# Expert weights in whole units of 2 MB, and hidden activations turned in 64x64 quarters, in a two-layer encoder on one core

## What is computed

```python
# t: tokens x 1024.  w_gate, w_up: 4 x 4 experts x 1024 x 512.  w_down: 4 x 4 x 512 x 1024
gates = g_onehot[:, :, None] * (g_w[:, None] * e_gate)[:, None, :]   # top group, then its top 2 experts
out = jnp.zeros_like(t)
for gi in range(MOE_GROUPS):
    hg = jnp.einsum('td,edf->tef', t, w_gate[gi])
    hu = jnp.einsum('td,edf->tef', t, w_up[gi])
    act = jax.nn.silu(hg) * hu * gates[:, gi, :, None].astype(t.dtype)
    out = out + jnp.einsum('tef,efd->td', act, w_down[gi])
```

## Time and profile before

| | us |
|---|---|
| median of 3 runs | 730.15 |
| lowest and highest of them | 729.17 and 730.3 |
| the profiled execution | 729.28 |
| its span, first to last instruction | 727.5 |

### The profile page before, as it was taken

One profiled execution on the slowest core, in us unless ns is written; L12 is line 12 of the kernel. 1 busy time (PEld: TensorE's weight loads), 2 busy tenths in 40 slices (PEclk: granted clock), 3 DMA queues, 4 the chain that ended last, 5 costly groups with the idle time before them and its releaser, 6 DMA issues.

```text
span 727.5 us, 8400 instructions
## 1 busy us (share of the span) xinstructions
PE 707.7 (97%) x3182; PEld 329.6 (45%) x3182; DVE 277.8 (38%) x683; ACT 149.2 (21%) x365; POOL 26.4 (4%) x47
## 2 busy tenths in 40 slices
PE   9999999999999999989999999999999999998996
PEld 6488454564333333333445545464333333332344
DVE  1213361544427242422322557363435424242224
ACT  3000241341111111110331144242111111110132
POOL 0600000000000000000000000000000000000000
PEclk9999999999999999999999999999999999999999
DMA  9997448869999999999999851569999999999941
GB/s 344 373 294 283 183 173 326 341 241 410 425 420 421 419 423 419 421 420 423 401 381 408 341 204 71 185 242 387 421 422 420 421 420 422 421 420 422 405 163 59
DMA packets 50666, 250.89 MB, mean 345 GB/s; under 512 B 4713, under 2 KB 5961, under 8 KB 26049
## 3 DMA queue, kind: packets, MB, share of 16 engines
q1 hardware_dynamic: 48256, 245.04, 84.1%
q0 software_dynamic: 2048, 5.07, 2.3%
q10 hardware_dynamic: 320, 0.22, 0.1%
HBM read 247.15 MB, written 4.73 MB: 346 GB/s over the span
## 4 chain that ended last, share of the span: by engine, by line
PE 85%; DMA 7%; issue 2%; SPq 2%; DVE 2%; ACT 1%; POOLq 0%; POOL 0%; ACTq 0%; DVEq 0%
PE bank L981 26%; PE bank L666 24%; PE bank L998 13%; DMA weights<-in_moe_w_down_dram 7%; PE bank L699 4%; PE bank L1019 4%; PE bank L941 2%; PE bank L893 2%; SPq L438 2%; PE bank L651 2%; PE bank L990 1%; PE bank L679 1%; PE bank L805 1%; PE bank L737 0%; PE bank L1241 0%
## 5 line engine op out<-in xcount | busy, mean ns | idle before, releaser
L981 PE MATMUL bank<-weights,expert_rows 128*64 128x512 f32 x1024 | 227.0, 593 | 6.8 <-DMA weights<-in_moe_w_up_dram 6.8
L666 PE MATMUL bank<-weights,normalised 128*128 128x512 f32 (+1 forms) x448 | 191.4, 580 | 0.9 <-DVE normalised L1637 0.7
L981 PEld LDWEIGHTS bank<-weights,expert_rows 128*64 128x64 f32 x1024 | 74.5, 137 | 149.9 <-issue 149.7
L666 PEld LDWEIGHTS bank<-weights,normalised 128*128 128x128 f32 x448 | 83.1, 190 | 91.4 <-issue 88.5
L998 PE MATMUL bank<-weights,hidden_turned_odd 128*64 128x512 f32 x256 | 58.8, 598 | 0.7 <-DMA weights<-in_moe_w_down_dram 0.7
L998 PE MATMUL bank<-weights,hidden_turned 128*64 128x512 f32 x224 | 51.5, 598 | 1.3 <-DVE hidden_turned L1957 0.6
L1477 ACT ACTIVATE gate_tanh<-bank 128x256 f32<-128x256 f32 x32 | 12.3, 384 | 190.5 <-PE bank L981 190.5
L1339 ACT ACTIVATE expert_outputs<-bank 128x512 fp32r<-128x512 f32 x32 | 19.1, 597 | 123.4 <-PE bank L998 123.4
L1987 DVE TENSOR_TENSOR gather_onehots<-bank,expert_outputs 128x512 fp32r<-128x512 f32 x32 | 22.1, 692 | 55.6 <-ACT expert_outputs L1339 55.5
L1957 DVE COPY hidden_turned<-bank 128x256 f32<-128x256 f32 x16 | 6.8, 424 | 78.5 <-PE bank L990 78.5
L1957 DVE COPY hidden_turned_odd<-bank 128x256 f32<-128x256 f32 x16 | 6.8, 425 | 78.2 <-PE bank L990 78.2
(11 more groups left out here) (265 smaller groups left out, 591.1 us busy)
## 6 DMA issues: line engine op xcount, KB each, us to landing
weights<-in_moe_w_gate_dram SPq DMA_DIRECT2D x64, 1024.0 KB, 16.0
weights<-in_moe_w_up_dram SPq DMA_DIRECT2D x64, 1024.0 KB, 16.9
weights<-in_moe_w_down_dram SPq DMA_DIRECT2D x60, 1024.0 KB, 19.8
weights<-in_even_w_in_dram SPq DMA_DIRECT2D x5, 2048.0 KB, 21.0
weights<-in_ple_w_gate_dram SPq DMA_DIRECT2D x4, 2048.0 KB, 31.3
weights<-in_even_w_out_dram SPq DMA_DIRECT2D x2, 2048.0 KB, 31.3
weights<-in_odd_w_qkv_dram SPq DMA_DIRECT2D x2, 2048.0 KB, 19.6
weights<-in_odd_w_out_dram SPq DMA_DIRECT2D x2, 2048.0 KB, 19.7
```

The costliest lines, as they stand in the source:

```text
L666: mm = pe.matmul(B[bank][:, 0:width], XT[:, k, tok(t)], w[:, k, :], start=(k == 0), stop=(k == KD - 1))
L981: mm = pe.matmul(bank[j * BLK:(j + 1) * BLK, :].rearrange("p (m f) -> p m f", m=2), rows[:, k, :], W[:, slots, a:a + FF // 2], start=(k == ...
```

## The change

For experts 7 to 13 of both layers each unit comes in one transfer of 2 MiB, with 16 KB unbroken in each partition. SyncE waits for the end of the slot's former unit ahead of it, and TensorE waits for all of it ahead of the product. Experts 0 to 6, 14 and 15 keep their halves.

So that a down matrix can lie unbroken too, every down matrix (of all experts) is now laid down with rows 4p to 4p + 3 in partition p. Step f of `down` then needs the hidden features 4p + f. These are columns f, f + 4, ... of `US` in each half j, turned: eight products of 64 partitions with 64 columns, in the two quarters of the array on its diagonal, into partitions 0 to 63 and 64 to 127 of bank 6.

```diff
@@ -52,11 +52,17 @@
 MOE_SLOTS = (2, 3, 4, 5, 6, 7, 8, 0, 1)
 BETWEEN_SLOTS, END_SLOTS = (4, 5, 6, 7, 8, 0, 1), (4, 5, 6)
 OUTSIDE = (U_MOE0 + 8, U_MOE1 + 8)
+WHOLE = (7, 14)
 
 
 def expert_units(u0):
 
     return [u0, u0 + 1] + [u0 + n for e in range(1, NE) for n in (3 * e, 3 * e + 1, 3 * e - 1)] + [u0 + 3 * NE - 1]
+
+
+def in_one(n):
+
+    return any(u0 + 3 * WHOLE[0] <= n < u0 + 3 * WHOLE[1] for u0 in (U_MOE0, U_MOE1))
 
 
 def place_units():
@@ -69,7 +75,7 @@
         last[s] = n
         firsts[s] += 16
         landed[n] = firsts[s]
-        if any(u0 <= n < u0 + 3 * NE for u0 in (U_MOE0, U_MOE1)):
+        if any(u0 <= n < u0 + 3 * NE for u0 in (U_MOE0, U_MOE1)) and not in_one(n):
             seconds[s] += 16
             second[n] = seconds[s]
 
@@ -424,8 +430,7 @@
                 if m < 2:
                     sp.dma_start(dst, s.rearrange("(p k) f -> p (k f)", p=P)).then_inc(done, 16)
                 else:
-                    sp.dma_start(dst.rearrange("p (j n) -> p j n", j=2), s.rearrange("(j p c) d -> p j (c d)", j=2, c=2))\
-                        .then_inc(done, 16)
+                    sp.dma_start(dst, s.rearrange("(p f) d -> p (f d)", p=P)).then_inc(done, 16)
 
             def experts(l, u0):
                 srcs = (wg_d, wu_d, wd_d)
@@ -434,7 +439,7 @@
                     if m < 2:
                         src = s.rearrange("(p k) f -> p (k f)", p=P)[:, half * 2048:(half + 1) * 2048]
                     else:
-                        src = s[256 * half:256 * half + 256, :].rearrange("(p c) d -> p (c d)", c=2)
+                        src = s.rearrange("(p f) d -> p (f d)", p=P)[:, half * 2048:(half + 1) * 2048]
                     sp.dma_start(dst, src).then_inc(done, 16)
 
                 def half_reusable(n, half):
@@ -452,12 +457,21 @@
 
                 def outside(f):
 
-                    s = srcs[2][l * NE + 2][256 * (f // 2):256 * (f // 2) + 256, :].rearrange("(p c) d -> p c d", c=2)
-                    sp.dma_start(H[:, f - 2, :], s[:, f - 2, :]).then_inc(sem("down2_rest_landed"), 16)
+                    s = srcs[2][l * NE + 2].rearrange("(p f) d -> p f d", p=P)
+                    sp.dma_start(H[:, f - 2, :], s[:, f, :]).then_inc(sem("down2_rest_landed"), 16)
+
+                def load_whole(e, m):
+
+                    n = u0 + 3 * e + m
+                    half_reusable(n, 1)
+                    load(srcs, l * NE + e, m, unit(n), landed(n)[0])
 
                 def load_down(e):
 
                     n = u0 + 3 * e + 2
+                    if in_one(n):
+                        load_whole(e, 2)
+                        return
                     for half in range(2):
                         half_reusable(n, half)
                         load_half(e, 2, n, half, (landed, second_landed)[half](n)[0])
@@ -479,7 +493,7 @@
                             sp.dma_start(side_product[l, :, 1, 512 * half:512 * half + 512], SIDE[1][half])\
                                 .then_inc(sem("side_second_stored"), 16)
                         sp.wait_ge(sem("side_second_stored"), 32 * (l + 1))
-                        sp.dma_start(XD[:, :], srcs[2][l * NE + 2][0:256, :].rearrange("(p c) d -> p (c d)", c=2))\
+                        sp.dma_start(XD[:, :], srcs[2][l * NE + 2].rearrange("(p f) d -> p (f d)", p=P)[:, 0:2 * D])\
                             .then_inc(sem("down2_landed"), 16)
                         sp.wait_ge(sem("seeded"), 4 * l + 2)
                         outside(2)
@@ -497,6 +511,10 @@
                         load_part(5, 1, 0)
                         load_part(5, 1, 1)
                         load_down(4)
+                    elif WHOLE[0] <= e < WHOLE[1]:
+                        load_whole(e, 0)
+                        load_whole(e, 1)
+                        load_down(e - 1)
                     elif e != 4:
                         for half in range(2):
                             for m in range(2):
@@ -986,8 +1004,10 @@
 
                 def turned_back():
 
-                    for c in range(2):
-                        mm = pe.transpose(B[6][:, c * P:(c + 1) * P], US[:, c:2 * P:2], ident)
+                    for f in range(KF):
+                        for j in range(2):
+                            r = slice(j * BLK, (j + 1) * BLK)
+                            mm = pe.matmul(B[6][r, f * BLK:(f + 1) * BLK], US[r, f:2 * P:KF], ident[r, r], start=True, stop=True)
                     return mm
 
                 def down(bank, hid, rows, second, halves):
@@ -995,7 +1015,7 @@
                         if f == KF // 2:
                             second()
                         for half in range(2):
-                            mm = pe.matmul(bank[half * BLK:(half + 1) * BLK, :], hid[:, 2 * (f % 2) + f // 2, :],
+                            mm = pe.matmul(bank[half * BLK:(half + 1) * BLK, :], hid[:, f, :],
                                            rows(f)[:, half * 512:(half + 1) * 512], start=(f == 0), stop=(f == KF - 1))
                         if f == KF // 2 - 1 and halves is not None:
                             mm.then_inc(halves, 1)
@@ -1035,8 +1055,9 @@
 
                 def wait_second(*ns):
                     for n in ns:
-                        s, w = second_landed(n)
-                        pe.wait_ge(s, w)
+                        if n in SECOND:
+                            s, w = second_landed(n)
+                            pe.wait_ge(s, w)
 
                 def second_half(e, n):
                     if e == NE - 1:
```

## The result

| us | before | after |
|---|---|---|
| median of the runs | 729.66 (4 runs) | 741.31 (4 runs) |
| lowest and highest | 728.91 and 730.3 | 740.77 and 767.97 |
| the profiled execution | 729.28 | 740.99 |
| its span | 727.5 | 739.2 |

The changed kernel is slower: ratio 1.0157, 95% interval 1.0138 to 1.0177. The run of 767.97 is no part of the ratio; its mean granted clock was 0.948, that of the other three 0.997 to 0.998. Forecast were 726.6 and a range of 723.0 to 730.4.

The account below looks back on a forecast made before the run. The weight transfer stream was taken to bound both expert stages, with TensorE nearly level. Longer runs gave -1.55 us a stage, -3.1 in all, other terms nothing: 726.6 us forecast, range 723.0 to 730.4.

Parts of the forecast that it names:

- What bounds the kernel: Both expert stages: the weight transfer stream sets the end; TensorE alone would be only 3.5 and 3.9 us earlier.
- Longer runs: Weight stream, experts 7 to 13: 16 KB packets take 613.5 ns instead of 622.6, gaining 1.55 us a layer.
- Later issue at no cost: Whole units wait until the slot's former unit is used up; the stream doesn't run dry at expert 7's gate: 0.
- Later landing: New waits of 1.4 and 1.9 us before expert 13 replace old ones before expert 15: cost 0.
- Other order of the down weights: Down matrices' halves stay 8 KB runs, now 16 KB apart, and land as fast as before: 0.
- The turned activations: Turning, 32 experts: eight quarter products take 0.38 us instead of 0.44, bringing nothing; up to 1.04 if quarters can't work together.
- Rival 3: Turned activations: quarters take turns in bank 6, 0.60 us more an expert, 741.1 us; chance 0.08.

Follow-up runs that it names:

- plain_full: The kernel before, its two full-array turning transposes written as plain float32 products with the identity: 729.47 us, ratio 1.0003.
- pair_columns: The changed kernel, but turned by two full-array products as before, with gate and up columns dealt in pairs to the array halves: 730.14 us, ratio 1.0015.
- dma_alone: The kernel before with only gate and up of experts 7 to 13 as whole units, old down layout and turning: 726.52 us, ratio 0.9964.
- packed: The changed kernel, but VectorE writes `US` so that the 64 columns a turning product loads lie side by side: 728.42 us, ratio 0.9985.
- half_turned: The changed kernel with four of the eight turning products left out: 727.82 us, ratio 0.9981.
- step_two: The changed kernel, but each turning product loads its 64 columns 2 elements apart instead of 4: 727.62 us, one run.
- turn_alone: The changed kernel with all transfers in halves, keeping the new down layout and the turning in quarters: 741.79 us, ratio 1.0169.

## Why the prediction was wrong

- *What bounds the kernel* was right: the stream, with 3.5 and 3.9 us of spare in TensorE. So was the point from which longer products decide, 0.22 us an expert: 0.23 (plain_full) changed nothing, 0.31 (pair_columns) cost 1.0 us, 0.66 cost 11.7.
- *Longer runs* were right: 613 ns a packet (613.5 forecast), 427 GB/s, a whole unit every 4.90 us (4.906), stage end 1.06 us earlier for 14 units in layer 0 of dma_alone (1.04).
- *Later issue at no cost* was right: in dma_alone expert 7's gate is issued at 208.24 and lands at 217.25, 4.89 us behind the half before it, so with no gap. In the changed kernel itself TensorE gives slots back later, and that distance is 5.3 us in layer 0 and 6.4 in layer 1; there the stream no longer sets the end.
- *Later landing* was right in place and size (1.69 and 1.58 us for 1.4 and 1.9), and free in dma_alone. It is free only while the stream sets the end. In layer 0 of packed the stage ended 1.1 us later than the sum has it with the turning at 0.60 (354.04 against 353.85 - 1.55 + 0.6 = 352.9), and that is the wait of 1.14 us.
- *Other order of the down weights* was put at 0 and was not 0: with it the stream reaches expert 7 about 0.6 us later (under packed). The loss doesn't hang on this term, since the stream doesn't set the end there. But the 1.55 us of 21 whole units a layer were never seen whole at a stage's end: counted from the stage's first expert product, the last down matrix landed 0.3 us later to 1.8 earlier than before in packed, half_turned, step_two and pair_columns.
- *The turned activations*, the term that failed: 0.38 us taken, 0.38 to 1.04 bounded, 1.10 measured. Two errors, which packed separates. First, the count. I took each product in the diff for one instruction and put the eight products into four groups; a plain float32 product is two instructions, so there are eight pairs: +0.23 us (0.61). The rows showed it: the sequence of TensorE's instructions shown with the change has 1 + 7 + 1 + 7 = 16 products for a `gate_up`, its row says x32, and the turning by `transpose` says x2 for two. The text ahead of the prediction makes the same mistake where it gives `gate_up` 32 products and `down` 16; they are 16 and 8 products of two instructions each. The price of a pair, 0.055 us, was right for columns side by side (0.058). Second, the step: the columns are 4 elements apart, and that doubles a pair: +0.49 us (1.10). The score products of the earlier trace rows load columns side by side, and I never asked whether these do.
- *Rival 3* named the place of the loss, and its size by luck, 741.1 against 741.31 measured: its 1.04 us stood for eight single quarters one after another at 0.11, the 1.10 are eight pairs at 0.12. Its mechanism didn't come about. The two quarters do run together in one bank (packed). So the Trainium skill's rule (TensorEngine Tiling (Array Packing), Gotcha 1: PSUM Pressure) doesn't hold for these diagonal quarters, which write different partitions of bank 6.
- The sum by the measured term: 0.66 x 16 = 10.6 us a layer, two layers less 3.5 and 3.9 are 13.7; 11.7 were measured. Where waits stood before products or in the middle of them, the steps were longer than the waits explain (expert 14 in layer 0: 12.46 us without its waits, against 12.04). Without the waits 0.7 to 0.8 us a layer come back, where the prediction has 0.28: from its first expert product to the scatter behind its last down product the stage grew by 6.4 us in layer 0 and 5.9 in layer 1. The rest is no effect of the change: in the profiled execution the first expert product started 0.6 us earlier than before (152.81 against 153.42), and over all runs' traces that start lies between 152.5 and 153.7.

The step was also there to be read. The Trainium skill (Advanced Engine Details and Errata, SBUF Cachelines) says that SBUF has cachelines of 16 bytes, that at least two hits on a line are needed to absorb its access latency, and that another line for each access is penalised. It gives no size. In float32 a step of 2 gives two hits a line, 3 gives 1.33, 4 gives one. The runs agree: 60, 88 and 120 ns are about 1, 1.5 and 2 times the 58 ns of columns side by side. The runs show the rate and not the lines, so the cause behind the rate is the page's.

## What to carry over

Count instructions by the trace's x-numbers and not by calls in the code: here a plain float32 product is two, a transpose one, and a new operation must be priced with its own count and its own column step. When two resources are nearly level, the spare is spent once: once longer products have used it, each late landing costs time, as in layer 0 of packed. A new layout has a price in the transfers too. Take a change with two halves apart first: whole gate and up units alone, with 16 KB runs and the old turning, are the fastest version (726.5 us, 0.9964 of before), and the half of the change that made room for 7 further units a layer cost 12.7 us by itself (turn_alone), nearly 5 times the 2.6 that dma_alone gained.

## What the runs showed of the hardware

- Weight loads of 64 float32 columns into 64 rows come every 58 to 60 ns at steps of 1 and 2 elements, every 88 at 3, and every 120 at 4 (134, 135, 171 and 210 ns each by the records). Into 128 rows a load takes 137 ns at step 1 and 200 at step 4. 128 columns at step 2 come every 118.
- Two 64x64 quarters on the array's diagonal work at once into one bank, with no cost seen: two instructions of 64 columns every 58 ns (packed), one of 128 columns in the full array every 118 (plain_full).
- A plain float32 product is two load and product instructions, a transpose one (plain_full against before: 4 and 2 for two products).
- On this queue packets of 2, 8 and 16 KB took 87, 309 to 312 and 613 ns. An estimate from these medians is 5 to 13 ns a packet beside its bytes; one from the rates, 421 GB/s in runs of 8 KB and 426 to 428 in runs of 16, is 7 to 10. The instruction fetches, also packets of 16 KB but of another queue, took 1.06 us (median) and said nothing about that.
- A single late landing stays in the stream: the whole unit that landed 1.5 us late at 278.29 in packed left all behind it late, though the bytes moved in each half microsecond around it show no break.
- 512 float32 columns moved in pairs, with pairs left out between them, and written in pairs, took 612 ns and not 593.
